# One block for the back half of an encoder layer: slot tables by one-hot products, fused layer norms, and the second expert product by halves of the output columns

## The reference, cut to what matters

```
h      = layer_norm(alpha * h + merged @ w_out, ln_mix_g, ln_mix_b)
scores = sigmoid(h @ router_w)                     # 512 x 32 experts, 8 groups of 4
sel    = scores + router_b
group  = argmax over groups of the sum of its two best sel
expert = the two best sel inside that group; gate = scores[expert] / their sum
y      = sum over the two of gate * ((silu(h @ w1[e]) * (h @ w3[e])) @ w2[e])
out    = layer_norm(alpha * h + y, ln_ffn_g, ln_ffn_b)
```

## Time and profile before

| | us |
|---|---|
| three runs | 1461.07, 1463.0, 1462.91 (median 1462.91) |
| the profiled execution | 1460.36 |
| its span in the trace | 1458.5 |
| PE busy | 1261.4 (86%) |
| DVE busy | 789.8 (54%) |
| ACT busy | 611.1 (42%) |
| POOL busy | 259.5 (18%) |

### The profile page before, as it was taken

How to read it: one execution, slowest core, us unless ns; L and a number is a source line. 1 busy time by engine, 2 the same in 40 slices (tenths; PEclk the granted TensorE clock), 3 DMA queues, 4 the chain that set the end, 5 groups by cost and what they waited for, 6 DMA issues and landing times. The chain is left out here.

```text
span 1458.5 us, 15122 instructions
## 1 busy us (share of the span) xinstructions
PE 1261.4 (86%) x5744; PEld 877.0 (60%) x5744; DVE 789.8 (54%) x918; ACT 611.1 (42%) x766; POOL 259.5 (18%) x230
## 2 busy tenths in 40 slices
PE   2998999869999999998899329999999999999930
PEld 1777877458887878777445226655666556665510
DVE  5684661474434344354422537777667776667607
ACT  4243333633423323231201136665666656666511
POOL 3222070003232323211001041111111111111003
PEclk9999999989999999999899559999999999999975
DMA  7221220102221202111670539999999999999414
GB/s 257 88 86 58 87 87 0 44 5 60 73 58 51 73 23 73 51 49 39 225 318 22 199 102 381 391 395 399 395 395 399 394 395 396 399 399 389 185 45 164
DMA packets 96510, 278.98 MB, mean 191 GB/s; under 512 B 8688, under 2 KB 58544, under 8 KB 71728
## 3 DMA queue, kind: packets, MB, share of 16 engines
q1 hardware_dynamic: 91056, 269.53, 49.5%
q0 software_dynamic: 5376, 8.42, 1.8%
HBM read 267.37 MB, written 18.94 MB: 196 GB/s over the span
## 5 line engine op out<-in xcount | busy, mean ns | idle before, releaser
L1974 DVE TENSOR_TENSOR wlo<-wraw,whi 128x2048 fp32r<-128x2048 f32 x128 | 287.6, 2287 | 46.6 <-ACT whi L1918 43.1
L1918 ACT ACTIVATE whi<-wraw 128x2048 fp32r<-128x2048 f32 x128 | 240.8, 1907 | 62.9 <-SPq L1803 34.1
L1888 PE MATMUL yb<-wraw,act_t 128*64 128x512 f32 x512 | 226.5, 595 | 1.3 <-issue 1.3
L1860 PE MATMUL hb<-whi,xs 128*128 128x512 f32 x512 | 211.4, 413 | 1.7 <-DVE xs L1978 1.5
L1861 PE MATMUL hb<-wlo,xs 128*128 128x512 f32 x512 | 201.9, 394 | 0.0
L384 PE MATMUL pj<-h_part,wsplit 128*128 128x512 f32 x672 | 166.5, 407 | 6.1 <-issue 3.4
L1152 PE MATMUL gate_ps<-h_part,gws 128*128 128x512 f32 x576 | 164.3, 421 | 2.3 <-ACT h L1295 2.3
L384 PEld LDWEIGHTS pj<-h_part,wsplit 128*128 128x128 f32 x672 | 129.7, 194 | 38.7 <-issue 10.6
L1888 PEld LDWEIGHTS yb<-wraw,act_t 128*64 128x64 f32 x512 | 67.5, 137 | 134.7 <-issue 132.7
L1860 PEld LDWEIGHTS hb<-whi,xs 128*128 128x128 f32 x512 | 97.1, 190 | 45.9 <-issue 27.3
L1152 PEld LDWEIGHTS gate_ps<-h_part,gws 128*128 128x128 f32 x576 | 103.6, 191 | 29.3 <-issue 12.2
(11 more groups left out here) (323 smaller groups left out, 1736.3 us busy)
## 6 DMA issues: line engine op xcount, KB each, us to landing
wraw<-in_moe_w SPq DMA_DIRECT2D x192, 1024.0 KB, 7.8
h<-in_w_in SPq DMA_DIRECT2D x14, 1024.0 KB, 5.5
h<-in_w_in SPq DMA_DIRECT2D x24, 512.0 KB, 4.5
h_dram<-h SPq DMA_DIRECT2D x8, 512.0 KB, 3.8
h<-in_w_branch SPq DMA_DIRECT2D x16, 256.0 KB, 2.7
kept_dram<-h SPq DMA_DIRECT2D x16, 256.0 KB, 2.1
wraw<-in_w_out SPq DMA_DIRECT2D x2, 2048.0 KB, 14.0
yr<-y_dram SPq DMA_DIRECT2D x4, 1024.0 KB, 10.6
```

The lines of the kernel that those rows point to most:

```text
L1860: pe.matmul(bank[:, :], lhs, whi[:, u % NSPLIT, cols], start=(half == 0 and kk == 0), stop=False)
L1888: last = pe.matmul(yb[c][0:SLOTS, :], act_t[:, k, :], raw[:, room, cols], start=(k == 0), stop=(k == FT - 1))
L1918: act.activation(whi[:, u % NSPLIT, :], raw[:, room, :], ACT.Copy).then_inc(S.hi_done, 1)
L1974: dve.tensor_tensor(wlo[:, u % NSPLIT, :], raw[:, room, :], whi[:, u % NSPLIT, :].bitcast(F32), ALU.subtract).then_inc(S.lo_done, 1)
```

## The change

`merge`, `experts` and `final` become one function `back` with one block. Its parts, and the core of the diff:

1. The norm is fused. PE transposes the tile before it is normalized, and the router's logits are corrected afterwards: the router's weights are multiplied by the gain and freed of their column mean beforehand, and the logits are scaled by 1/std and get a bias. The norm itself is two three-operand DVE instructions with a per-partition scalar (`scaled`, `shifted`); ACT gives only the root, and POOL has no part. The last tile's `shifted` stands after the slot table's first part in DVE's list.
2. PE's list puts each `turn` and `logits` between the halves of the projection.
3. The slot tables: DVE builds one-hot matrices (128 tokens x 64 slots) and a table of row numbers (128 tokens x 2 x 32), and PE sums the eight products; DVE turns the result into `rows_all`. The eight scatters, the table in DRAM and its reading back go. The few linked steps of the choice of experts are paired with independent ones. What serves the further experts (`spare_rows`, `spare_experts`, eight small products) and the gates stand inside the rounds of experts 1 to 3.
4. The gates are applied at the end, to y read back, divided by alpha (epsilon of the last norm is divided by alpha squared).
5. The second product goes one half of the columns at a time, each over the whole contraction. Both w2 rooms become free only after the second half; ACT copies the first half while PE makes the second.
6. The last gain and bias are loaded during the experts; the branch around the further experts stands in each engine's list. SP waits for the scatters, branches, and loads y.

```diff
-                        sp.wait_ge(S.w2_used, 2 * eb + hb_ + 1)
+                        wait(sp, S.w2_used, 2 * eb + 2)
                     else:
-                        sp.wait_ge(S.lo_done, split_unit(eb, before, hb_) + 1)
+                        wait(sp, S.lo_done, split_unit(eb, before, hb_) + 1)
...
-            def second_products(e, half):
-                room, landed = place_of(units, "w2", e, half)
-                pe.wait_ge(S.w_in[room], landed)
-                if half == 0:
-                    pe.wait_ge(S.act_done, e + 1)
-                    wait(pe, S.y_ready, 2 * e)
-                for kk in range(2):
-                    k = 2 * half + kk
-                    for c in range(2):
-                        cols = slice(kk * DM + c * 512, kk * DM + c * 512 + 512)
-                        last = pe.matmul(yb[c][0:SLOTS, :], act_t[:, k, :], raw[:, room, cols], start=(k == 0), stop=(k == FT - 1))
-                last.then_inc(S.w2_used, 1)
+                last.then_inc(S.h3_turned.sem, 1)
+
+            def second_products(e, c):
+                if c == 0:
+                    wait(pe, S.act_done, e + 1)
+                wait(pe, S.y_ready, 2 * (e - 1) + c + 1)
+                for k in range(FT):
+                    room, landed = place_of(units, "w2", e, k // 2)
+                    if c == 0 and k % 2 == 0:
+                        wait(pe, S.w_in[room], landed)
+                    cols = slice(k % 2 * DM + c * 512, k % 2 * DM + c * 512 + 512)
+                    last = pe.matmul(yb[c][0:SLOTS, :], act_t[:, k, :], raw[:, room, cols], start=(k == 0), stop=(k == FT - 1))
+                last.then_inc(S.w2_used.sem, 1)
...
-            def weigh_y(e):
...
+            def take_y(e):
                 wait(act, S.scattered[e % 2], 16 * (e // 2))
-                gate = rows_all[:, first + e, 2:3].bitcast(F32)
                 for c in range(2):
-                    act.activation(ys[:, e % 2, c * 512:c * 512 + 512], yb[c][0:SLOTS, :], ACT.Copy, scale=gate).then_inc(S.y_ready, 1)
+                    wait(act, S.w2_used, 2 * e + c + 1)
...
+                sp.wait_ge(branch_done, KT)
+                for t in range(NT):
+                    sp.dma_start(h2[:, t, :], v["h_dram"][t * P:(t + 1) * P, :]).then_inc(h_in[t], 16)
+                for t in range(NT):
+                    if t == NT - 1:
+                        sp.wait_ge(out_done, 2 * NT)
+                        first_weights(sp, range(6, 8))
+                    sp.wait_ge(h2_ready, t + 1)
+                    sp.dma_start(v["h2_dram"][t * P:(t + 1) * P, :], h2[:, t, :]).then_inc(h2_out, 16)
+                first_weights(sp, range(8, NRAW))
...
+                left = blocks_left(sp)
+                all_scattered(sp, S, NE)
+                with sp.If(left > 0):
+                    sync_program(sp, S2, OVER, further, 0)
+                    all_scattered(sp, S2, OVER)
+                for t in range(NT):
+                    sp.dma_start(yr[:, t, :, :], v["y_dram"].rearrange("(s q) d -> s q d", q=2)[t * P:(t + 1) * P, :, :]).then_inc(y_in[t], 16)
+                for t in range(NT):
+                    sp.wait_ge(o_ready, t + 1)
+                    sp.dma_start(v["out"][t * P:(t + 1) * P, :], h2[:, t, :]).then_inc(out_stored, 16)
+                sp.wait_ge(out_stored, 16 * NT)
...
+                for t in range(NT):
+                    project(t, 0)
+                    if t >= 1:
+                        turn(t - 1)
+                    if t == 2:
+                        pe.wait_ge(router_set, 1)
+                    if t >= 2:
+                        logits(t - 2)
+                    if t < NT - 1:
+                        project(t, 1)
+                    else:
+                        project(t, 1, range(4))
+                        logits(t - 1)
+                        project(t, 1, range(4, KT))
+                turn(NT - 1)
+                logits(NT - 1)
+
+                pe.wait_ge(mask_done, 1)
+                pe.matmul(cp[:, 0:TE], cn("before"), mask.rearrange("p t e -> p (t e)"), start=True, stop=False)
+                pe.wait_ge(earlier_done, 4)
+                pe.matmul(cp[:, 0:TE], ones, earlier[:, 0:NT, :].rearrange("p t e -> p (t e)"), start=False, stop=True)
+                pe.matmul(cp[:, TE:TE + NE], ones, earlier[:, NT, :], start=True, stop=True).then_inc(pos_done, 1)
+                pe.wait_ge(table_done, 1)
+                for i in range(2 * NT):
+                    if i % NT == 0:
+                        pe.wait_ge(place_done, i // NT + 1)
+                    last = pe.matmul(cp[0:SLOTS, AT_ROWS:AT_ROWS + 2 * NE], place_one[:, i, :],
+                                     table[:, i, :, :].rearrange("p c e -> p (c e)"), start=(i == 0), stop=(i == 2 * NT - 1))
+                last.then_inc(rows_summed, 1)
...
+                def between(e):
+                    if e == 2:
+                        pe.wait_ge(spare_done, 1)
+                        for i in range(2 * NT):
+                            last = pe.matmul(cp[0:SLOTS, AT_SPARE:AT_SPARE + 2 * OVER], spare_one[:, i, :],
+                                             spare_table[:, i, :, :].rearrange("p c b -> p (c b)"), start=(i == 0), stop=(i == 2 * NT - 1))
+                        last.then_inc(spare_summed, 1)
+
+                tensor_program(pe, S, NE, between)
...
+                    if t == NT - 1:
+                        copy_turned(0)
+                    act.wait_ge(stats_ready, t + 1)
+                    act.activation(rstd[:, t:t + 1], mv[:, t, 1:2], ACT.Sqrt, bias=epsc[:, 0:1]).then_inc(std_ready, 1)
+                    if t < NT - 1:
+                        copy_turned(0)
+                    copy_turned(1)
...
+                def scaled(t):
+                    chain.add(dve.scalar_tensor_tensor(h2[:, t, :], h2[:, t, :], mv[:, t, 0:1], lng, ALU.subtract, ALU.mult))
+
+                def shifted(t):
+                    dve.scalar_tensor_tensor(h2[:, t, :], h2[:, t, :], rstd[:, t:t + 1], lnb, ALU.mult, ALU.add).then_inc(h2_ready, 1)
+
+                for t in range(NT):
+                    dve.wait_ge(h_in[t], 16)
+                    residual(t, 0)
+                    if t == NT - 1:
+                        for before in range(t):
+                            router_logits(before)
+                    residual(t, 1)
+                    dve.wait_ge(res_done, 2 * t + 2)
+                    for half in range(2):
+                        chain.add(dve.bn_stats(stats[:, t, half, :], h2[:, t, 512 * half:512 * half + 512]))
+                    chain.wait()
+                    dve.bn_aggr(mv[:, t, :], stats[:, t, :, :]).then_inc(stats_ready, 1)
+                    dve.wait_ge(stats_ready, t + 1)
+                    dve.wait_ge(std_ready, t + 1)
+                    chain.link(dve.reciprocal(rstd[:, t:t + 1], rstd[:, t:t + 1]))
+                    if t == 0:
+                        dve.wait_ge(ln_in, 32)
+                    dve.wait_ge(turned, 2 * t + 2)
+                    scaled(t)
+                    if t < NT - 1:
+                        chain.wait()
+                        shifted(t)
+                router_logits(NT - 1)
...
+                ki = onek[:, :, :, :].rearrange("p k t e -> p (k t) e")
+                row = cn("row").rearrange("p (i c) -> p i c", c=2)
+                for c in range(2):
+                    chain.add(dve.tensor_tensor(table[:, :, c, :], ki, bc(row[:, :, c], 2, NE), ALU.mult))
+                chain.wait()
+                dve.sem_inc(table_done, 1)
+                shifted(NT - 1)
+                dve.wait_ge(pos_done, 1)
+                pos = cp[:, 0:TE].rearrange("p (t e) -> p t e", t=NT)
+                for k in range(2):
+                    chain.add(dve.tensor_tensor(pk[:, NT * k:NT * k + NT, :], onek[:, k, :, :], pos, ALU.mult))
+                chain.wait()
+                chain.link(dve.tensor_reduce(posk, pk, AX.X, ALU.add))
+                for k in range(2):
+                    i = slice(NT * k, NT * k + NT)
+                    dve.tensor_tensor(place_one[:, i, :], bc(posk[:, i], 2, SLOTS), bc(cn("count"), 1, NT), ALU.is_equal).then_inc(place_done, 1)
+
+                wait(dve, S.hi_done, 1)
+                dve.wait_ge(turn_copied, 2 * NT)
+                dve.tensor_tensor(wlo[:, 0, :], raw[:, 0, :], whi[:, 0, :].bitcast(F32), ALU.subtract).then_inc(S.lo_done.sem, 1)
+                dve.wait_ge(rows_summed, 1)
+                dve.tensor_scalar(rows_all[:, :, 0:NE], cp[0:SLOTS, AT_ROWS:AT_ROWS + 2 * NE].rearrange("s (c e) -> s c e", c=2),
+                                  float(FAR), None, ALU.add).then_inc(rows_done, 1)
...
+                def spare_rows():
+
+                    blocks = SEQ // SLOTS - 1
+                    chain.add(dve.tensor_tensor(more_e, bc(cp[:, TE:TE + NE], 2, blocks), bc(cn("steps"), 1, NE), ALU.is_gt))
+                    chain.link(dve.tensor_tensor(more_k, bc(posk, 2, blocks), bc(cn("steps"), 1, 2 * NT), ALU.is_ge))
```

(49 more changed lines are left out.)

772 lines of the change are left out of this document (360 added, 412 removed).

## The result

The changed kernel takes 1425.59 us (median of 4 runs, 1424.19 to 1426.86) against 1462.95 us before (4 runs, 1461.07 to 1463.39): ratio 0.9747, 95% interval 0.973 to 0.9764. The profiled execution took 1426.86 us, its span is 1425.1 us, and the mean granted clock rose from 0.944 to 0.956. In that execution the unchanged front ended 3.2 us later than in the trace of before (the back half's first product starts at 712.9 us against 709.7), so stages are compared by their lengths.

A forecast was written before the change was run, and what follows sets the result against it. PE was taken to bound the expert rounds, with gains only before and after them. Terms of -6.7, -1.3, -22.1, +6.3, -0.6, -7.3, -1.0 and -5.1 sum to -37.8 us: 1425 on the median's footing, range 1412 to 1440.

The forecast's parts named there:

- The likeliest case: Whole kernel: the prediction's own case, a time of 1420 to 1430 us, given 58%.
- last token tile to the choice: Last token tile up to the sigmoid: the choice begins at 811.0 instead of 817.72, -6.7 us.
- choice of experts: DVE's small linked instructions: pairing leaves 12 links, 4.6 us instead of 5.9, -1.3 us.
- mask to gather: Slot table, from mask to gather: 9.1 us instead of 31.2, -22.1 us.
- gather to first product: From the gather's start to the first expert product: kept at 10.5 us, between -5 and +5.
- rounds of the experts: Expert stage: DVE's spare work stalls PE and PE gets 16 records more, +6.3 us, bounds 0 and 10.
- first copy, gap before y, landing of y: After the last expert: copy under PE -0.6, drain and meetings gone -7.3, first y tile lands sooner -1.0 us.
- four tiles of the tail: From first y tile to the end: 28.0 us on DVE alone instead of 33.1, -5.1 us.
- the step named for that case: Slot table: `low(0)`, 2.29 us on DVE, would be late next if PE's eight products took under 2.3 us.
- PE stalls of 2.5 and 1.8 us with hand-overs: Expert rounds: PE waits caused by `spare_rows` (4.4 us) after round 1 and `spare_experts` (3.7 us) after round 3.
- The rival that blamed them: Gather late behind four weight loads or tile 3's store, DVE delays at full length: +5 and +3, 1433 us; 12%.
- The w2 rooms: Expert rounds: w2 rooms freed 3.4 us later starve PE of weights, up to +47, 1510 us; 3%.

The follow-up runs named there:

- Experiment 4: Changed kernel, but DVE normalizes each token tile before PE turns it, with plain router weights and no logits correction: 1431.00 us.
- experiment 1: Changed kernel with spare_rows and spare_experts moved ahead of sum_h1 in rounds 1 and 3, where DVE waits for PE: 1416.61 us.
- experiment 2: Changed kernel with seven added DVE delays of 4 to 12 linked statistics ahead of the sum of h3, after rounds 7 to 25: 1456.82 us.
- Experiment 7: Changed kernel, but SP issues the ring's last four weight loads only after the first two gathers have landed: 1421.59 us.
- experiment 3: Changed kernel, but SP takes the branch around the further experts before it waits for the scatters: 1423.53 us.
- Experiment 5: Changed kernel with the last norm shared again: ACT normalizes, DVE multiplies by the gain, POOL adds the bias: 1432.83 us.
- Experiment 6: Changed kernel with the second product again by halves of the contraction, each freeing its w2 room: 1425.65 us.

## Why the prediction was right, and where it was not

The forecast was 1425.0, the result 1425.6. The likeliest case came true, but one term was too small by 4.5 us, and the others together gained 3.5 us more than forecast. That the forecast lies 0.6 us from the result is in part luck. Lengths from the two traces, in us:

| step of the prediction | predicted | measured |
|---|---|---|
| last token tile to the choice | -6.7 | -7.7 |
| choice of experts | -1.3 | -1.4 |
| mask to gather | -22.1 | -23.1 |
| gather to first product | 0 | +0.4 |
| rounds of the experts | +6.3 | +10.8 |
| first copy, gap before y, landing of y | -0.6 -7.3 -1.0 | -10.5 |
| four tiles of the tail | -5.1 | -5.3 |
| sum | -37.8 | -36.8 |

The medians differ by 37.4 us. The table's sum and the 3.2 us by which this trace's front is longer make the 33.4 us between the spans, but for 0.2 of rounding.

- *Last tile.* Right in kind: the last residual 4.5 us later, 4.9 us on to the choice instead of 5.5. Experiment 4 shows that it is the raw turn that pays.
- *Slot table.* The one-hot products took 0.12 us a record, not the 0.215 priced from the earlier trace rows; what came next was the step named for that case, `low(0)`. Of the 1.5 us saved on PE only 1 came through.
- *Rounds.* This is the step that failed. "PE stalls of 2.5 and 1.8 us with hand-overs" was right (2.71 and 1.83), and "PE itself gets 16 records, 2.0 us" was high: the round that holds them is 1.2 us longer. What was left out is that PE's clock falls in a stall. "Nothing gives this back" is true, but something adds to it: 2.77 and 1.70 us, removed by experiment 1 together with the stalls and made again by experiment 2. The prediction had the price in view, logits at half clock behind PE's waits in the earlier trace rows, and used it only where PE had long been idle. Of the remaining 0.6 us, 0.45 lie in the first round (17.04 us before, 17.49 after, from the first product to the first second product): it starts at half clock in both traces, for 8 of its records before and 11 after. What lengthened that was not tried.
- *Gather.* Kept at 10.5 us, measured 10.9. Experiment 7 shows that 4 of them were the weight loads beside it. The rival that blamed them had the mechanism right and its +5 wrong: from gather to turning it took 7.85 us before the change too, where loads were issued 1 us behind it (what part they had there was not tried), and 8.3 after.
- *Gap before y.* 5.29 us from scatter to load where 6.25 was charged: the landing was right, and the branch is 2.66 us and not the 3.65 read from the earlier trace rows (experiment 3). y lands 4.95 us after its issue, not 5.5.
- *Tail.* Instructions of 1.28 us as priced, 6.93 us a tile. Experiment 5 shows that the gain comes from POOL's absence and not from fewer instructions, and that POOL's drain, which the earlier trace rows showed at the end of the experts, would come back at the end of the kernel if POOL had a last step there.
- *The w2 rooms.* Experiment 6 closes this rival from both sides: no gain, no loss.

## What to carry to other kernels

In a stage bound by PE, small work on another engine costs nothing where it fits into that engine's own gap: read where it waits for PE and put the work right there, since two places in one list some 8 us apart differed by 9 us. By these traces a stall of PE of 1.5 us or more is to be priced at its length and 1.4 to 2.9 us of half clock, with some chance of none. A wait and a slow step that don't depend on each other, as the branch and the scatter, or the gather and loads needed much later, are worth reordering even late in tuning.
